# Differential attention on one core: order of the score products, and one row-maximum instruction for both half heads

## The reference

```python
def diff_attend(q, k, v, lam):
    """q (B, Lq, H, 2, d), k (B, Lk, H, 2, d), v (B, Lk, H, 2d) -> (B, Lq, H, 2d)."""
    s = jnp.einsum("bqhpd,bkhpd->bhpqk", q, k).astype(jnp.float32) * (HEAD_DIM_2 ** -0.5)
    p = jax.nn.softmax(s, axis=-1)
    a = p[:, :, 0] - lam * p[:, :, 1]
    return jnp.einsum("bhqk,bkhe->bqhe", a.astype(v.dtype), v)
```

## Time and profile before

| | before |
|---|---|
| median of 3 runs | 3706.11 us |
| lowest, highest | 3705.8, 3707.85 us |
| the profiled execution, its own time | 3702.62 us |
| its span in the trace | 3700.9 us |
| mean granted TensorE clock over the span | 0.95 |
| TensorE, VectorE, ScalarE busy | 91%, 49%, 29% of the span |

### The profile page before, as it was taken

The page is one execution under the profiler, slowest core; times in us unless marked ns, Lnnn a source line. Parts: engine busy times, 40 slices in busy tenths (PEclk is TensorE's granted clock), DMA queues, the critical chain, the costliest instruction groups (busy, mean ns, idle before and its releaser), DMA issues. The chain is left out here.

```text
span 3700.9 us, 39086 instructions
## 1 busy us (share of the span) xinstructions
PE 3374.5 (91%) x16274; PEld 2716.8 (73%) x16274; DVE 1829.7 (49%) x2297; ACT 1084.2 (29%) x1416; POOL 1208.2 (33%) x354
## 2 busy tenths in 40 slices
PE   7999999999989998999995897977999989889998
PEld 6988778777777777798882485956788766358886
DVE  5655493848473525357454246464322465343224
ACT  3222333332323322232222315243322331032322
POOL 3333442524142433333330120302444342034443
PEclk8999999999999999899995899999999999999999
DMA  4444321212121232355451110201233232013321
GB/s 151 160 148 159 112 76 50 74 49 74 43 80 52 86 102 70 108 176 171 137 160 36 46 63 1 69 1 46 85 97 97 86 114 91 0 46 95 99 92 68
DMA packets 278289, 321.08 MB, mean 87 GB/s; under 512 B 6866, under 2 KB 243041, under 8 KB 277922
## 3 DMA queue, kind: packets, MB, share of 16 engines
q1 hardware_dynamic: 239808, 245.38, 20.6%
q10 hardware_dynamic: 38306, 73.20, 5.9%
HBM read 312.27 MB, written 6.29 MB: 86 GB/s over the span
## 5 line engine op out<-in xcount | busy, mean ns | idle before, releaser
L297 POOL TENSOR_TENSOR Wl<-Wr,Wh 128x2048 fp32r<-128x2048 f32 x232 | 1069.4, 4610 | 1930.4 <-ACT Wh L962 1930.4
L435 PE MATMUL ps<-Ah,Wh 128*128 128x512 f32 x2048 | 831.1, 406 | 81.0 <-POOL Wl L297 38.6
L436 PE MATMUL ps<-Al,Wh 128*128 128x512 f32 x2048 | 811.0, 396 | 0.0
L437 PE MATMUL ps<-Ah,Wl 128*128 128x512 f32 x2048 | 810.3, 396 | 0.0
L962 ACT ACTIVATE Wh<-Wr 128x2048 fp32r<-128x2048 f32 x232 | 442.8, 1909 | 426.4 <-PE ps L437 418.5
L435 PEld LDWEIGHTS ps<-Ah,Wh 128*128 128x128 f32 x2048 | 392.4, 192 | 197.9 <-POOL Wl L297 55.6
L436 PEld LDWEIGHTS ps<-Al,Wh 128*128 128x128 f32 x2048 | 393.1, 192 | 84.2 <-issue 5.8
L437 PEld LDWEIGHTS ps<-Ah,Wl 128*128 128x128 f32 x2048 | 392.3, 192 | 84.7
L435 PE MATMUL ps<-Yh,Wh 128*128 128x512 f32 x1088 | 425.1, 391 | 3.4 <-POOL Wl L297 3.4
L437 PE MATMUL ps<-Yh,Wl 128*128 128x512 f32 x1088 | 424.1, 390 | 0.0
L436 PE MATMUL ps<-Yl,Wh 128*128 128x512 f32 x1088 | 423.8, 390 | 0.0
(11 more groups left out here) (292 smaller groups left out, 3981.9 us busy)
## 6 DMA issues: line engine op xcount, KB each, us to landing
Wr<-in_a_w_in_dram SPq DMA_DIRECT2D x48, 1024.0 KB, 5.2
modw<-in_w_mod_dram ACTq DMA_DIRECT2D x96, 512.0 KB, 4.5
Wr<-in_b_w_in_dram SPq DMA_DIRECT2D x40, 1024.0 KB, 5.0
Wr<-in_w_mlp_in_dram SPq DMA_DIRECT2D x32, 1024.0 KB, 5.6
Wr<-in_w_mlp_out_dram SPq DMA_DIRECT2D x32, 1024.0 KB, 5.2
Wr<-in_a_w_out_dram SPq DMA_DIRECT2D x16, 1024.0 KB, 5.2
Wr<-in_c_w_in_dram SPq DMA_DIRECT2D x16, 1024.0 KB, 5.6
Wr<-in_attn_w_qkv_dram SPq DMA_DIRECT2D x12, 1024.0 KB, 5.1
```

Of the source, the lines that this page charges most:

```text
L297: pool.tensor_tensor(E.Wl[:, s, :], E.Wr[:, s, :], E.Wh[:, s, :].bitcast(F32), ALU.subtract).then_inc(*LO.did(p))
L435: pe.matmul(o, ah, bh, start=first, stop=False)
L436: pe.matmul(o, ah, bl, start=False, stop=False)
L437: return pe.matmul(o, al, bh, start=False, stop=last)
```

## The change

TensorE's order within the scores of a unit becomes: half 0's 512 columns, half 1's 512 columns, half 0's 256, half 1's 256. All four banks are waited for ahead of the first product, and one event comes at the end instead of one for each half. VectorE takes the maxima of both halves with one instruction on a view of 2 x 768 columns, and scales both with one. Both exponentials wait for this one event.

```diff
-            for p in range(2):
-                into(4 + 2 * p)
-                into(5 + 2 * p)
-                q = QD[64 * p:64 * p + 64, h, j * P:(j + 1) * P]
-                c = 2 * p * S
-                pe.matmul(psf[:, c:c + S], q, KDt[64 * p:64 * p + 64, h, 0:S], start=True, stop=True)
-                pe.matmul(psf[:, c + S:c + NK], q, KDt[64 * p:64 * p + 64, h, S:NK], start=True, stop=True).then_inc(*X.did("D", "s", i, u, p))
-                emptied[4 + 2 * p] = emptied[5 + 2 * p] = A.of("D", "exp", i, u, p)
+            for b in range(4, 8):
+                into(b)
+            for c0, c1 in ((0, S), (S, NK)):
+                for p in range(2):
+                    m = pe.matmul(psf[:, 2 * p * S + c0:2 * p * S + c1], QD[64 * p:64 * p + 64, h, j * P:(j + 1) * P],
+                                  KDt[64 * p:64 * p + 64, h, c0:c1], start=True, stop=True)
+            m.then_inc(*X.did("D", "s", i, u))
+            for b in range(4, 8):
+                emptied[b] = A.of("D", "exp", i, u, b // 2 - 2)
...
-            act.wait_ge(*V.of("D", "nm", i, u, p))
+            act.wait_ge(*V.of("D", "nm", i, u))
...
-            for p in range(2):
-                c = 2 * p * S
-                dve.wait_ge(*X.of("D", "s", i, u, p))
-                dve.tensor_reduce(stD[:, o + p:o + p + 1], psf[:, c:c + NK], AX.X, ALU.max).then_inc(*V.did())
-                dve.wait_ge(*V.now())
-                dve.tensor_scalar(stD[:, o + 2 + p:o + 3 + p], stD[:, o + p:o + p + 1], -0.125, None, ALU.mult).then_inc(*V.did("D", "nm", i, u, p))
+            dve.wait_ge(*X.of("D", "s", i, u))
+            dve.tensor_reduce(stD[:, o:o + 2], psf.rearrange("p (a n) -> p a n", a=2)[:, :, 0:NK], AX.X, ALU.max).then_inc(*V.did())
+            dve.wait_ge(*V.now())
+            dve.tensor_scalar(stD[:, o + 2:o + 4], stD[:, o:o + 2], -0.125, None, ALU.mult).then_inc(*V.did("D", "nm", i, u))
```

## The result

The changed kernel takes 3727.86 us, the median of 5 runs (3725.34 to 3728.73), against 3706.11 (3705.8 to 3708.43): 21.75 us more, a ratio of 1.0058 with the 95% interval 1.0046 to 1.0069. The forecast was 3727, in a range of 3719 to 3746.

What follows compares the result with a forecast made beforehand. The prediction took the loops to be bound by a chain of waits through VectorE's maxima, half 1's exponential and VectorE's combination. Series 20.2, absorbed -2 and clock +3 gave +21 us, a median of 3727 us, range 3719 to 3746.

Steps and rivals of the forecast that it cites:

- What bounds the loop: Two loops: a chain of VectorE's maxima, half 1's exponential on ScalarE and VectorE's combination, 5.45 us a unit; TensorE outside it.
- The maximum: VectorE's single instruction over 1536 columns takes 1.75 us, bounds 1.60 and 1.90; the two before took 1.90.
- The series: Unit head: both exponentials follow the one maximum, reciprocals at 3.88 instead of 3.25; +0.63 us in 32 units, 20.2 us.
- the bounds on ScalarE: Second exponential starts 0.89 us after the first, at most 0.99 if it must wait for the accumulator's read.
- TensorE's order and waits at nothing: Next unit's scores start at 3.97, take 1.63 us and stay hidden with 0.5 us of cover; no gain from order.
- What is absorbed: At scalings of finished heads, VectorE's waits for TensorE's spread hide the increase; 2 us off, three places.
- The clock: Loops: TensorE idles more, so six more falls to half speed at about 0.5 us; +3 us, bounds 0 and 12.
- rival of a lasting low clock: TensorE at half speed through the loops: +58 us, 3764; over a third of units 3739; 13% for +30 or more.
- The sum: Whole kernel: 20.2 - 2 + 3 = +21 us, median 3727 us, 0.57% slower.
- Savings count: Rival: VectorE's 0.3 us saved a unit falls on the path; gain 10 us, 3696 us; 5%.
- Halves don't overlap in the new order: Rival: scores take 2.6 us and TensorE ends each unit, 1.1 us a unit; 35 us, 3741 us; 8%.

Runs made afterwards that it cites:

- e4: Kernel before plus two unused VectorE multiplications (0.84 us a unit) ahead of the wait for the second exponential; 3707.56 us, ratio 1.0005.
- e5: Kernel before, with half 0's reciprocal and scaling moved into VectorE's wait for the second exponential; 3686.31 us, ratio 0.9945 to the kernel before.
- e2: Kernel before with only VectorE's part of the change: one maximum and one scaling after the second event, TensorE as before; 3731.32 us, ratio 1.0069.
- e8: Kernel before, still two maxima, but the first exponential also waits for the second half's maximum; 3732.79 us, ratio 1.0073.
- e1: Changed kernel with a maximum, scaling and event for each half again, TensorE's part kept; 3707.58 us, ratio 1.0005 to the kernel before.
- e3: Changed kernel with the four score products back in the old order, half 0's two then half 1's; 3729.3 us, ratio 1.0063 to the kernel before.

## Why the prediction was right

**What bounds the loop** was right in every link: VectorE's maxima, the second exponential, VectorE's combination. e4 shows the wait as free room, e5 the stretch behind it as path.

**The maximum.** 1.75 us by the slope of the earlier trace rows; measured 1747 to 1758 ns, with a median of 1751, over 32.

**The series.** +0.63 a unit; the reciprocals went from 3.25 to 3.90 and regular intervals from 5.45 to 6.09 or 6.10, +0.645 on the mean, 20.6 us for 20.2. Of the bounds on ScalarE, 0.89 and 0.99, the lower one held. VectorE waits 1.94 us before the reciprocals; the forecast's 2.05 doesn't follow from its own times, by which the scaling ends at 1.94 and the wait at 3.88, so 1.94. This term is the result; e2 and e8 isolate it.

**TensorE's order and waits at nothing.** Right: e1 and e3. The scores start at 4.12 for 3.97 and take 1.56 us for 1.63, so the cover was 0.42 us for 0.5.

**What is absorbed.** The sum of 2 us was right, the count behind it wrong, which is luck. Only four of the eight scalings of a head have a maximum behind them in their pass, not six. These four intervals took 7.50 and three times 8.61 us before, and 8.61, 8.14, 8.62 and 8.61 after: 0.65 more where 4 x 0.64 would be 2.56, so 1.9 us absorbed. It depends on the clock: the stretches of 8.61 and 8.62 have a granted clock of 0.80 in both kernels, and there VectorE's wait for TensorE's spread L478 shrinks (from 1.02 us at 2277.10 to 0.38 at 2260.30 after the change); at 1.00 a stretch takes 7.50 before and 8.14 after. Two of them, the first from the kernel before, and the wait in a slow one after the change:

```profile
2272.12:2280.73 8.61, 6.20 (x34) 5.25 (x34) 5.70 (x12) 3.10 (x6) 0.00 (x0) 0.80 0.00 0
...
2284.10:2292.24 8.14, 4.64 (x34) 3.69 (x34) 5.40 (x10) 2.99 (x6) 0.00 (x0) 1.00 0.00 0
...
2260.30 0.75 DVE L1885 SCALAR_TENSOR_TENSOR acc<-acc,GC,ps 128x512 f32<-128x512 f32 x1 [0.38 <-PE ps L478]
```

**The clock.** Over-sized: I added 3 us for more falls. Outside those four intervals, one fall lengthened an interval before (6.33 us, by 0.88) and two after: 7.10, by 1.01, and 7.09, by 1.14, as this one is the first of its pass, which takes 5.95 undisturbed. That is 1.3 us more. Not every longer interval is a fall: one in each kernel (5.80 before, 6.45 after) is 0.35 longer at a granted clock of 1.00, where VectorE's copy starts late for a reason that the profile doesn't show:

```profile
2274.56 0.42 DVE L1877 COPY tmp<-ps 128x256 f32<-128x256 f32 x1 [0.27 <-issue]
```

A fall that meets the scores looks as reckoned: passes of 2.93 us (2.9 in the forecast), and the maximum late by 0.91. From the changed kernel's timeline:

```profile
2220.36 2.93 PE L781 MATMUL psx<-KDt,QD 64*128 64x512 f32 x8 [2.44 <-ACT rs L1290]
...
2223.34 1.76 DVE L1837 TENSOR_REDUCE stD<-psx 128x2 f32<-128x1536 f32 x1 [0.91 <-PE psx L781]
```

TensorE idled longer in each unit (busy 61.86 of 101.76 us against 70.44 of 92.22) and was yet granted about the same clock. The rival of a lasting low clock didn't come true.

**The sum.** 20.6 - 1.9 + 1.3 = 20.0 us, which is what the two loops and their last units show. Between the medians lie 21.75, with an interval of 17 to 26 by the ratio's, so the remaining 2 us are within the noise and aren't explained further. That the forecast of 3727 lies within 1 us of the measured median is therefore luck in part: a clock term 1.7 us too large stands where this remainder is. Spans of single executions shouldn't be subtracted for this: those of the two traces differ by 25.2 us, of which 3.9 had passed before the first maximum (2206.38 and 2210.29), in code that the change doesn't touch.

**Rivals.** "Savings count" fell with the result, which is no faster: the 0.3 us saved lie inside the longer series, and e4 shows that the wait behind them was free room. "Halves don't overlap in the new order" fell with the 1.56 us.

The Trainium skill, "TensorE: Matmul & The Clock Gate", the section on packing small matmuls, has matmuls start strictly in program order. This case's traces don't agree: e3, in the old order, takes 1.57 us for eight passes, and in the first unit before the change all four passes of L782, half 1's too, start ahead of the first pass of L783, though half 0's L783 was issued before half 1's L782.

## What to carry to other kernels

Before merging two small instructions into one, ask what runs between them: here the first one's result started another engine, and the merge turned two overlapped steps into a series, 0.65 us in each of 32 units, while the busy times of VectorE and TensorE fell. Work just ahead of a wait is free as long as what ends the wait doesn't depend on it; work moved from behind the wait into it is worth its full length (20 us here, and 38 with the scaling of the maxima folded away). A cover can be gone at the next step: the late start of the scores cost nothing in regular units of the changed kernel, and it bound them once VectorE's path was shortened.

## What the hardware showed that was not expected

ScalarE started an exponential 0.89 us after another one that writes its row sum, though the first one's accumulator was read only until 0.99. Products on rows 0 to 63 and on rows 64 to 127 of the array ran together in either program order, eight passes in 1.56 and 1.57 us. And a VectorE maximum over a view of 2 x 768 PSUM columns, with the 256 columns between left out, cost the same 1.04 ns a column as the operations, with one fixed part for both rows.
